# Token rows for the experts made by ScalarE in the output layer; a row gather at every second unit of the query layer; three raw slots, five pairs of half buffers, ten row buffers

## The reference, cut to what matters

```python
h = h + (g_attn * y_attn + g_rnn * y_rnn) @ w_out          # output layer
x = rms_norm_2(h, ffn_norm)                                  # x * rsqrt(mean(x*x) + eps) * gain
q = (x @ w_peer_q).reshape(B, S, 8, 2, 128)                  # query layer
s = einsum('bshcd,hcnd->bshcn', q, subkeys)                  # 2 x 128 scores per head
top_s, top_i = lax.top_k(s, 16)
cand = top_s[..., 0, :, None] + top_s[..., 1, None, :]       # 256 sums per head
best_s, best_c = lax.top_k(cand, 16)                         # 16 experts per token and head
gates = softmax(best_s)
u = peer_u[experts]                                          # 256 x 128 rows of 2048 floats
act = gelu(einsum('tkd,td->tk', u, x))
y = einsum('tk,tkd->td', gates * act, peer_v[experts])       # as many rows of peer_v
h = h + y
h = h + sigmoid(rms_norm_2(h, ple_norm) @ w_ple_gate) * (p @ w_ple_proj)
return rms_norm_2(h, final_norm)
```

## Time and profile before

| | |
|---|---|
| median of 3 runs | 3846.93 us (3846.39 to 3849.86) |
| the profiled execution | 3850.2 us, span 3848.4 us, mean granted TensorE clock 0.925 |
| TensorE products | 3278.8 us busy, 85% |
| VectorE | 2473.9 us, 64% |
| ScalarE | 1422.3 us, 37% |
| GpSimd | 865.4 us, 22% |
| DMA | 952.86 MB; 248 GB/s mean |

### The profile page before, as it was taken

The page is one execution under the profiler, slowest core; times in us unless marked ns, Lnnn a source line. Parts: engine busy times, 40 slices in busy tenths (PEclk is TensorE's granted clock), DMA queues, the critical chain, the costliest instruction groups (busy, mean ns, idle before and its releaser), DMA issues.

```text
span 3848.4 us, 53065 instructions
## 1 busy us (share of the span) xinstructions
PE 3278.8 (85%) x20976; PEld 2731.2 (71%) x20976; DVE 2473.9 (64%) x3286; ACT 1422.3 (37%) x2046; POOL 865.4 (22%) x627
## 2 busy tenths in 40 slices
PE   8988898999999999999999996766666667666678
PEld 8988887999999999999998996632222223222248
DVE  6577765654455556875546667877777776555566
ACT  6445555553354444664445452221000001100025
POOL 2000011000000100000000021245665565555532
PEclk9999999999999999999999997888788888888899
DMA  6433243555555565455452456899999999999964
GB/s 229 151 105 121 94 159 110 176 185 185 178 186 185 185 206 169 160 186 182 166 181 92 159 186 224 315 360 421 422 421 422 421 421 420 422 422 421 421 286 148
DMA packets 188024, 952.86 MB, mean 248 GB/s; under 512 B 20992, under 2 KB 21120, under 8 KB 121984
## 3 DMA queue, kind: packets, MB, share of 16 engines
q0 software_dynamic: 73728, 536.90, 33.8%
q1 hardware_dynamic: 114048, 412.56, 32.0%
HBM read 947.29 MB, written 2.10 MB: 247 GB/s over the span
## 4 chain that ended last, share of the span: by engine, by line
PE 56%; DMA 19%; DVE 14%; POOL 4%; ACT 4%; issue 3%; DVEq 0%; ACTq 0%; SPq 0%; POOLq 0%
PE ps L537 55%; DMA BIG<-in_peer_v,CS 7%; DMA HLF<-in_peer_v,CS 7%; DVE HL L1766 3%; DMA HF<-in_peer_v,CS 2%; POOL BIG L519 2%; POOL HLF L519 2%; DVE BIG L2410 2%; DVE BIG L1770 2%; DMA HLF<-in_peer_u,CS 1%; DVE BIG L1766 1%; ACT HL L1134 1%; ACT BIG L1128 1%; DMA BIG<-in_peer_u,CS 1%; DVE BIG L1762 0%
## 5 line engine op out<-in xcount | busy, mean ns | idle before, releaser
L537 PE MATMUL ps<-HS,HL 128*128 128x256 f32 x10128 | 1340.8, 288 | 36.0 <-DVE HL L1766 30.6
L537 PEld LDWEIGHTS ps<-HS,HL 128*128 128x128 f32 x10128 | 1287.4, 196 | 44.9 <-DVE HL L1766 34.4
L1766 DVE TENSOR_TENSOR HL<-RAW,HL 128x1024 fp32r<-128x1024 f32 (+1 forms) x772 | 954.1, 1236 | 244.6 <-ACT HL L1134 180.1
L1134 ACT CAST HL<-RAW 128x1024 fp32r<-128x1024 f32 (+1 forms) x772 | 805.5, 1043 | 497.1 <-PE ps L537 427.4
L537 PE MATMUL ps<-BIGR,HL 128*128 128x256 f32 x6720 | 894.8, 285 | 23.8 <-DVE HL L1766 15.2
L537 PEld LDWEIGHTS ps<-BIGR,HL 128*128 128x128 f32 x6720 | 851.0, 193 | 32.3 <-issue 15.7
L537 PE MATMUL ps<-BIG,HF 128*128 128x512 f32 (+1 forms) x744 | 391.1, 675 | 191.4 <-DMA BIG<-in_peer_v,CS 167.4
L537 PE MATMUL ps<-HLF,HF 128*128 128x512 f32 x648 | 342.6, 682 | 157.2 <-DMA HLF<-in_peer_v,CS 145.2
L537 PEld LDWEIGHTS ps<-BIG,HF 128*128 128x128 f32 (+1 forms) x744 | 159.0, 224 | 418.2 <-issue 384.0
L2410 DVE CUSTOM_DVE_ANT_0 BIG<-BIG 128x2048 f32<-128x2048 f32 x133 | 305.0, 2293 | 168.2 <-DMA BIG<-in_peer_u,CS 159.2
L482 POOL COPY NSUM<-TMP 128x256 f32<-128x256 f32 x6 | 3.3, 554 | 1747.9 <-ACT TMP L1130 1747.9
(11 more groups left out here) (198 smaller groups left out, 2237.9 us busy)
## 6 DMA issues: line engine op xcount, KB each, us to landing
RAW<-in_w_up SPq DMA_DIRECT2D x128, 512.0 KB, 3.4
RAW<-in_w_down SPq DMA_DIRECT2D x128, 512.0 KB, 4.2
RAW<-in_w_out SPq DMA_DIRECT2D x64, 512.0 KB, 4.1
RAW<-in_w_qk SPq DMA_DIRECT2D x32, 512.0 KB, 3.5
RAW<-in_w_xbc SPq DMA_DIRECT2D x32, 512.0 KB, 3.8
RAW<-in_w_xr SPq DMA_DIRECT2D x32, 512.0 KB, 3.3
RAW<-in_w_yr SPq DMA_DIRECT2D x32, 512.0 KB, 3.4
RAW<-in_w_gr SPq DMA_DIRECT2D x32, 512.0 KB, 3.4
```

What stands on the lines that cost most here:

```text
L537: return e.matmul(o, l, r, start=start, stop=stop, skip_group_check=True)
L1134: s.done(e.copy(o, i), sig)
L1766: v.done(e.tensor_tensor(o, a, b, op), sig)
```

## The change

Six things are changed together.

1. NRAW goes from 5 to 3 and NPAIR from 4 to 5. Casts run one unit further ahead: `high(u + 4)`, `low(u + 3)`.
2. HK moves to `chunks(15104, 16)` and is made during w2_out by ScalarE, as X times the gain *without* RX. Six of eight groups of transposes and copies into HN follow during w2_out, the last two at units 1 and 2 of w_pq.
3. Since HN and PQ no longer hold RX, the two halves of RX are turned into two columns RXC (one number per token). ScalarE multiplies the scores by it when it copies them, as two instructions instead of one, and gives it as scale to gelu. ScalarE, not VectorE, now evacuates the query chunks.
4. VectorE's `beside` does a step of `experts` at every unit until the first route is found, and at every second unit after that. The first route is spread over units, four steps at each.
5. The row buffers are ten (NPAIR gives one more): four for gathers 0 to 15, five for 16 to 25, ten after that. V rows begin after the 19th u row and follow at 240 to 238.
6. The steps of `experts` go on in w2_pp; the gates wait for its end.

The diff, cut to these:

```diff
-NRAW = 5
-NPAIR = 4
+NRAW = 3
+NPAIR = 5
...
-        PQ, SK, HK = chunks(8192, 8), big(10240, 2048), chunks(14336, 16)
-        ROWS = [big(12288 + 2048 * i, 2048) for i in range(4)] + [HF[:, 0, 0:2048]] + [HLF[:, i, :] for i in range(4)]
+        PQ, SK, HK = chunks(8192, 8), big(10240, 2048), chunks(15104, 16)
+
+        RXC = SM[:, 420:422]
+        ROWS = [big(12288 + 2048 * i, 2048) for i in range(4)] + [HF[:, 0, 0:2048]] + [HLF[:, i, :] for i in range(NPAIR)]
...
-            while vs and a >= 16 * vs[0][1] + 17 and (256 - len(vs)) * 224 < (a - 31) * 240:
+            while vs and a >= 16 * vs[0][1] + 17 and (256 - len(vs)) * 238 < (a - 17) * 240:
...
-            b = q % 4 if q < 32 else (q + 2) % 5 if q < 42 else (5, 6, 7, 8, 4, 0, 1, 2, 3)[(q - 42) % 9]
+            b = q % 4 if q < 16 else (q + 3) % 5 if q < 26 else (5, 6, 7, 8, 9, 4, 0, 1, 2, 3)[(q - 26) % 10]
...
 # TensorE
+                for j in range(4):
+                    yield from until(*(("w2_out", 4 * j + 6) if j < 3 else ("w_pq", 1)))
+                    for i in range(2):
+                        pe.wait_ge(s_hk, 4 * j + 4)
+                        turned([HK[:, c, i * 128:i * 128 + 128] for c in range(4 * j, 4 * j + 4)], TURN["rows"] + 2 * j + i)
+                        yield
+                columns(RX, RXN["ffn_norm"], TURN["ffn"])
+                yield
+
+            g_row = rows()
+            dense(L["w2_out"], cut_by(mix, s_mix, lambda k: k + 1), None, g_row)
...
 # ScalarE
-                        high(u + 3)
+                        high(u + 4)
...
+            def evac_out(c):
+                bank_done(L["w2_out"], c)
+                normed_high("ffn_norm", "ffn_norm", c)
+                act(HK[:, c, :], X[:, c, :], ACT.Identity, (s_hk, c + 1), scale=vec("ffn_norm", c))
...
-                    copy(SC[:, :, 2 * h:2 * h + 2, :], score_bank(k).rearrange("p (i c n) -> p i c n", i=2, c=2),
-                         sig_score(k))
-                    yield
+                    s.wait_ge(s_tfree, TURN["ffn"] + 1)
+                    for i in range(2):
+                        act(SC[:, i, 2 * h:2 * h + 2, :].rearrange("p c n -> p (c n)"), score_bank(k)[:, i * T:i * T + T],
+                            ACT.Identity, sig_score(k) if i else None, scale=RXC[:, i:i + 1])
+                    yield
...
             def evac_pq(c):
+                s.wait_ge(s_mm, L["w_pq"].done(c))
+                if c >= 8:
+                    s.wait_ge(s_score, SCORE["score"] + c // 2 - 3)
+                copy(PQ[:, c % 8, :], bank(L["w_pq"], c)[:, 0:T], sig_bank(L["w_pq"], c))
                 pq[0] = c + 1
...
-                    act(d, d, ACT.Gelu_apprx_tanh, (s_gact, n + 1))
+                    act(d, d, ACT.Gelu_apprx_tanh, (s_gact, n + 1), scale=RXC[:, n // 8:n // 8 + 1])
...
 # VectorE
-                        low(u + 2)
+                        low(u + 3)
...
-            def rows():
-                v.wait_ge(s_mm, L["w2_out"].end())
-                for c in range(16):
-                    stt(HK[:, c, :], X[:, c, :], vec("ffn_norm", c), RX, ALU.mult, ALU.mult, (s_hk, 1) if c == 15 else None)
-                    if c % 4 == 3:
-                        yield
-                for _ in range(4):
-                    yield
-                rowed[0] = True
...
-                while not rowed[0]:
-                    yield
...
                                 step(routes)
+                                steps += 1
+                                if steps % 4 == 0 and not routed[0]:
+                                    yield
...
             def beside():
+                turns = 0
                 while True:
                     step(g_row)
-                    step(g_row)
-                    step(g_ex)
+                    if found[0] == 0 or turns % 2:
+                        step(g_ex)
+                    turns += 1
                     yield
 
             def evac_pq(c):
-                if c >= 8:
-                    v.wait_ge(s_score, SCORE["score"] + c // 2 - 3)
-                scaled(PQ[:, c % 8, :], L["w_pq"], c)
                 pq[0] = c + 1
 
             dense(L["w_pq"], evac_pq, beside())
-            routed[0] = True
             v.wait_ge(s_phi, 1)
             tt(pin[1], PTF, pin[0].bitcast(F32), ALU.subtract, (s_pin, 1))
-            dense(L["w2_pp"])
+            dense(L["w2_pp"], None, g_ex)
+            routed[0] = True
             drain(g_ex)
```

More of the change, by code:

```diff
@@ L364, in build @@
         s_sk, s_p = sem("subkeys_in"), sem("p_in")
-        s_row = [sem(f"rows{i}_in") for i in range(9)]
+        s_row = [sem(f"rows{i}_in") for i in range(5 + NPAIR)]
         s_store = [sem(f"out{i}_stored") for i in range(4)]
@@ L1035, in scoring @@
                     yield
-            g_row, g_sc = rows(), scoring()
+            g_sc = scoring()
             def beside():
                 while True:
-                    step(g_row)
                     step(g_row)
@@ L1057, in value @@
                     pe.wait_ge(s_sfree[1], SCORE["score"] // 2 + 4)
-                    pe.wait_ge(s_tfree, TURN["rows"] + 8)
+                    pe.wait_ge(s_tfree, TURN["ffn"] + 1)
                     pe.wait_ge(s_ofree, OUTS["mla"] + 16)
@@ L1150, in dense @@
                     block, part = L.order[u - L.unit0]
-                    if L.name != "w2_pp" or u + 3 < L.unit0 + L.units:
-                        high(u + 3)
+                    if L.name != "w2_pp" or u + 4 < L.unit0 + L.units:
+                        high(u + 4)
                     if part == L.parts - 1:
@@ L1645, in scalar @@
             s.wait_ge(s_qp, 8)
-            dense(L["w2_out"], residual("ffn_norm", L["w2_out"]))
-            norm_end("ffn_norm", L["w_pq"])
             def rows():
-                for _ in range(4):
-                    yield
-                for i in range(2):
-                    for j in range(4):
-                        t = TURN["rows"] + 4 * i + j + 1
+                for j in range(4):
+                    yield from until(*(("w2_out", 4 * j + 6) if j < 3 else ("w_pq", 1)))
+                    for i in range(2):
+                        t = TURN["rows"] + 2 * j + i + 1
                         s.wait_ge(s_turn, t)
                         copy(HN[:, i, 512 * j:512 * j + 512], tr_bank, (s_tfree, t))
-                        if j % 2:
-                            yield
+                        yield
[4 more added lines that the diff above has]
+                act(HK[:, c, :], X[:, c, :], ACT.Identity, (s_hk, c + 1), scale=vec("ffn_norm", c))
+            g_row = rows()
+            dense(L["w2_out"], evac_out, g_row)
+            norm_end("ffn_norm", L["w_pq"])
             def scoring():
@@ L1801, in dense @@
                     block, part = L.order[u - L.unit0]
-                    if L.name != "w2_pp" or u + 2 < L.unit0 + L.units:
-                        low(u + 2)
+                    if L.name != "w2_pp" or u + 3 < L.unit0 + L.units:
+                        low(u + 3)
                     if part == L.parts - 1:
@@ L2337, in vector, with rows @@
             dense(L["w2_ao"], evac_ao, g_ml)
-            dense(L["w2_out"], residual("ffn_norm", L["w2_out"]))
-            norm_end("ffn_norm", L["w_pq"])
-            def rows():
-                v.wait_ge(s_mm, L["w2_out"].end())
-                for c in range(16):
-                    stt(HK[:, c, :], X[:, c, :], vec("ffn_norm", c), RX, ALU.mult, ALU.mult, (s_hk, 1) if c == 15 else None)
-                    if c % 4 == 3:
-                        yield
-                for _ in range(4):
-                    yield
-                rowed[0] = True
+            def rows():
+                for j in range(4):
+                    yield from until(*(("w2_out", 4 * j + 6) if j < 3 else ("w_pq", 1)))
+                    yield
+                    yield
+                columns(420, TURN["ffn"])
+                yield
+            g_row = rows()
+            dense(L["w2_out"], residual("ffn_norm", L["w2_out"]), g_row)
+            norm_end("ffn_norm", L["w_pq"])
             def top16(vals, v16, i16):
@@ L2408, in dot @@
                 i, h = divmod(n, 8)
+                v.wait_ge(s_tfree, TURN["rows"] + 8)
                 row, sig = arrived(q)
```

34 lines of the change are left out of this document (14 added, 20 removed).

## The result

The changed kernel takes 3816.22 us (median of 4 runs, 3815.2 to 3820.93) against 3847.73 for the kernel before (4 runs, 3846.39 to 3849.86): ratio 0.992, 95% interval 0.9903 to 0.9937. The profiled execution took 3816.82 us, its span is 3815.0. The forecast was 3814.

What follows compares the result with a forecast made beforehand. TensorE was taken to bound until 2313 us, VectorE the query layer, DMA from 2540 to 3720. The 3848.4 span less 26.9 and 6 gives 3815.5, execution 3817.3, median 3.3 lower: 3814 us; range 3793 to 3842.

Steps and rivals of the forecast that it cites:

- (a): Output layer: ScalarE's HK and HN work hidden; six transpose groups cost TensorE 4 us, so w2_out ends at 2317.3.
- (b): Start of the query layer: first gather near 2347.5, ten microseconds earlier; TensorE stands 2 to 3 us, not 12.7.
- (c): Rest of the query layer: TensorE just ahead as the bound; w2_pp begins at 2439.6, 64 us earlier.
- (d): At w2_pp 16 gathers are out, not 31; fifteen more cost 37.3 us; last row 26.9 us earlier.
- (e): Three raw slots, five half pairs: fewer TensorE waits before 2313; 6 us gained, bounds 25 gained and 12 lost.
- The sign that I named against myself: Before 2313 us: the prediction is wrong if ScalarE's casts wait for DMA there; no size given.
- (f): Last layer, after 3723.9 us, three preloaded units instead of five: 0, plus or minus 3 us.
- the last term: Whole kernel: the median of the runs lies 3.3 us below the profiled execution, turning 3817.3 into 3814.
- more gained: Rival: no TensorE weight waits in the query layer, fifth pair removes most residual waits; 50 to 58 us gained; chance 0.13.
- starvation ahead of the query layer: Rival: three slots starve TensorE before 2313, in attention, state-space and recurrence layers; 58 us lost, 3878 in all; chance 0.14.
- The slow query layer: Rival: query layer stays at half clock, 4.7 us a unit; 3848 in all, no change; chance 0.11.
- The change does not act: Rival: fetching rows half as often only defers them, costing 37.3 us, if the query layer does not shorten; no separate chance.

Runs made afterwards that it cites:

- e4: Changed kernel with nine row buffers instead of ten, the fifth half pair not used for rows: 3820.6 us, ratio 0.9918.
- e8: Changed kernel with the first gathers on two buffers, then three and four, so two rows go out at once instead of four: 3818.6 us, ratio 0.9917.
- e9: Changed kernel with ScalarE, in the query layer alone, copying query chunk and scores before casting the unit four ahead: 3817.6 us, ratio 0.9909.
- e11: Changed kernel with all ten buffers from gather 21 (e7) and ScalarE's copy ahead of its cast in the query layer (e9): 3813.3 us, ratio 0.9901.
- e3: Changed kernel with an expert step at every query-layer unit instead of every second, buffers and gates adapted, ten buffers: 3817.8 us, ratio 0.9920.
- e1: Kernel before with three raw slots, five pairs of half buffers and casts one unit further ahead, nothing else: 3841.0 us, ratio 0.9974.
- e10: Kernel before with three raw slots instead of five, nothing else: 3852.0 us, ratio 1.0003.
- e2: Changed kernel with five raw slots and four pairs as before, so nine row buffers: 3822.2 us, ratio 0.9931.
- e7: Changed kernel with all ten row buffers from gather 21 instead of 26: 3810.8 us, ratio 0.9894.

## Why the prediction was right

The time, 3816.2 against 3814, and the signs are right. By step:

- *(a) Rows in the output layer.* The transposes took 0.60 us each on TensorE, 3.6 in all (4 forecast), and ScalarE's work was hidden. Right.
- *(b) Start.* First gather 30.2 us after the layer's first product forecast, 29.95 measured. TensorE's stand behind it was forecast at 2 to 3 us and was 1.95, but a 4.88 us wait ahead of it and one of 5.55 behind it had not been: I had let only VectorE hold up a unit. In the trace VectorE's routing and its wait for the first row (8.32 us) also held the slots, so loads went out late, and ScalarE's cast, waiting for its load, held up the query copy.
- *(c) Layer.* 122.3 us forecast, 125.9 measured, within its bounds, by two errors that partly cancel. To the end of the last scoring it was 117.2 forecast and 123.3 measured. The wait for the p load behind it was put at 5.1 and was 2.6; the same wait is 4.5 to 4.9 in e4, e8, e9 and e11, so this part is luck. The pace was right, 13.2 us forecast for four units and a scoring and 13.13 measured from 2376 on. The 7 us for late weights were wrong in kind: I spread them over the layer at 0.33 us a unit. In the trace all of the loss, 16.8 us with the slow clock in it, lies ahead of 2376, behind slots that VectorE freed late; (b) and this term together had some 9.5 for it. That the clock would be near 1.0 was wrong: 0.92.
- *(d) Fewer rows.* 1257.4 us to the last row forecast, 1257.25 measured. e3 shows the exchange directly. That it is right to 0.2 us is luck: 17 gathers were out and not 16, so 14 rows were deferred, 34.9 us at 2.49, and not 37.3. Of the other 2.3 us about 1.1 lie in the first 36 us behind the layer, which ran at 278 GB/s against 291 before; the rest is not explained. My rest was 1379.7, measured 1383.2.
- *(e) Slots.* 6 us forecast; 6.5 less in the profiled front with 3.6 of transposes in it, so 10; e1 against e10 has 9.3, and the kernels with and without the pair in the change differ by 6 on average (2307.8 of nine, 2314.0 of two). The reason was right; the size is right by the last comparison and 3 to 4 too low by the others, since I had charged three raw slots with a loss that e10 does not find. The sign that I named against myself, ScalarE's casts waiting for loads in the front, occurred (26.7 us in w_up in the changed kernel) and meant nothing, as those waits replace waits for TensorE.
- *(f) The end.* 0.5 us longer; right.

The sum is better than its parts. The layer was forecast 3.6 us too short and the front 4.5 too late (2311.3, that is 2317.3 less 6, against 2306.8), and with the end's 0.5 the span came out at 3815.0 against 3815.5. That is luck. The 2 us by which the median is off come from the last term: I took it to lie 3.3 us below the profiled execution, as before, and it lay 0.6 below.

One slip in the rivals: "more gained" adds to 48 to 58 us, which from 3846.9 is 3789 to 3799, not 3791 to 3799. And the Trainium skill's formula ("DMA: Bandwidth & Descriptors", "Anatomy of one DMA") is its fit for transfers issued from GpSimd; the prediction used it for a weight load too, which SP issues. Nothing in the forecast hangs on it.

Of the rivals, starvation ahead of the query layer is out by e10. In the query layer it exists (24.4 us of ScalarE's waits), and e2 puts its price at 1.2 us in the rest and 3.3 in the layer, little more than what such lengths repeat to. The slow query layer did not come. Of the signs against me, the stretch at full rate read 419 GB/s from 2470 to 3688, just under 420, but 422 from 2500 to 3600, where e4 and e7 have 421. "The change does not act" is true of one part of it: fetching at every second unit, with the new slots and the changed kernel's buffers, is worth 0.2 us (e3).

## What to carry to other kernels

When a stage that is bound by transfers follows one bound by an engine, price each row fetched early at its transfer time and at what it costs the engine: here 2.7 us on either side, so the pace was nearly free to choose, and the gain lay in stalls at the start and in buffers that were free but not in the rotation. Where a ring of load slots is emptied by an engine that also has other work in its list, place that work by what it does to the next load, not only to the next product. An engine's wait for a load is only a loss if nothing downstream has slack; ask where the extra buffer goes, to the load or to the finished operand, and test each alone.

## What the runs showed of the hardware

Identical instruction streams up to the query layer reached it between 2305.9 and 2310.1 us in nine executions, a scatter as large as some of the effects; lengths inside one trace separated them where medians could not. A weight of 512 KB asked for while no row was on its way was in after 3.3 us (e8, 2332.2 to 2335.5), and one asked for with rows on their way after 7.4 us (the changed kernel, 2351.23 to 2358.65). A short wait of TensorE can cost twice, once as idle time and once as half clock behind it: the scoring that came after a wait of 4.88 us took 2.08 us instead of 1.13, and a unit some 13 us later, after one of 1.95 us, 4.63 instead of 2.88. In e9, where the first of these waits is missing, a wait of 4.79 us is followed by a unit of 4.63. How much each wait by itself has to do with the clock was not tried. The Trainium skill ("TensorE: Matmul & The Clock Gate", section "What's actually happening") has the clock at one of two levels. The scoring's 1.84 times agrees with the lower one over nearly all of it, the unit's 1.6 times with the lower one over a part.
